# Expert down product as three passes of the rounded format, with w_down split ahead of the expert stage

## What is computed

```
for e in range(N_EXPERTS):
    h = jax.nn.silu(xt @ w_gate[e]) * (xt @ w_up[e])
    out = out + comb[:, e:e + 1] * (h @ w_down[e]).astype(f32)
```

## Time and profile before

| | us |
|---|---|
| median of 3 runs | 1359.34 |
| lowest and highest | 1359.04, 1362.73 |
| the profiled execution | 1360.82 |
| its span, first to last instruction | 1359.2 |

### The profile page before, as it was taken

The page is one execution under the profiler, slowest core; times in us unless marked ns, Lnnn a source line. Parts: engine busy times, 40 slices in busy tenths (PEclk is TensorE's granted clock), DMA queues, the critical chain, the costliest instruction groups (busy, mean ns, idle before and its releaser), DMA issues. The chain is left out here.

```text
span 1359.2 us, 22656 instructions
## 1 busy us (share of the span) xinstructions
PE 1198.9 (88%) x6653; PEld 957.0 (70%) x6654; DVE 893.2 (66%) x1975; ACT 462.5 (34%) x696; POOL 486.3 (36%) x557
## 2 busy tenths in 40 slices
PE   7999999799979768999999269999999999999910
PEld 6997999778767534888888257767767767767600
DVE  3452866468877573466667667777777777777586
ACT  4121010110012451222221225556556555556433
POOL 3008850210110033322322233545545545445267
PEclk9999899899979998999999579999999999999965
DMA  8555352564155322433332546787877777644484
GB/s 257 172 199 156 105 166 63 145 231 183 63 154 157 104 96 67 152 112 112 120 119 98 223 164 192 216 244 225 253 203 227 211 210 217 144 98 98 112 318 171
DMA packets 112875, 222.84 MB, mean 164 GB/s; under 512 B 51305, under 2 KB 68281, under 8 KB 103569
## 3 DMA queue, kind: packets, MB, share of 16 engines
q1 hardware_dynamic: 96368, 164.86, 36.3%
q0 software_dynamic: 15408, 55.12, 17.5%
q10 hardware_dynamic: 1040, 2.10, 0.4%
HBM read 144.34 MB, written 77.58 MB: 163 GB/s over the span
## 5 line engine op out<-in xcount | busy, mean ns | idle before, releaser
L2057 DVE TENSOR_TENSOR wgu<-w_raw,wgu (+1 forms) x192 | 226.0, 1219 | 52.5 <-ACT wgu L2144 52.5
L2244 PE MATMUL p_gu<-wgu,xg_high 128*128 x768 | 254.5, 413 | 4.5 <-DVE xg_low L2050 4.5
L2144 ACT CAST wgu<-w_raw (+1 forms) x192 | 187.1, 1050 | 19.4 <-SPq L1865 16.7
L2244 PEld LDWEIGHTS p_gu<-wgu,xg_high 128*128 128x128 f32 x768 | 145.2, 191 | 59.1 <-issue 31.3
L2267 PE MATMUL p_d<-wd,ht 128*128 x384 | 174.9, 598 | 1.8 <-DVE ht L2071 1.0
L2244 PE MATMUL p_gu<-wgu,xg_low 128*128 x384 | 152.0, 396 | 0.0
L2267 PEld LDWEIGHTS p_d<-wd,ht 128*128 128x128 f32 x384 | 69.0, 189 | 71.5 <-issue 71.2
L1730 PE MATMUL p_out<-w_out_high,mixt_high 128*128 128x512 f32 (+1 forms) x272 | 108.6, 399 | 10.5 <-POOL mixt_low L1507 10.5
L1730 PE MATMUL p_out<-w_out_high,mixt_low 128*128 128x512 f32 (+1 forms) x272 | 106.9, 393 | 0.0
L1730 PE MATMUL p_out<-w_out_low,mixt_high 128*128 128x512 f32 (+1 forms) x272 | 106.8, 393 | 0.0
L1936 POOL TENSOR_TENSOR spare_e<-nothing 128x1 f32<-128x1 f32 x48 | 9.3, 194 | 232.2 <-DVE yo L2077 232.2
(11 more groups left out here) (434 smaller groups left out, 2689.0 us busy)
## 6 DMA issues: line engine op xcount, KB each, us to landing
w_raw<-in_w_gate SPq DMA_DIRECT2D x16, 1024.0 KB, 4.8
w_raw<-in_w_up SPq DMA_DIRECT2D x16, 1024.0 KB, 7.7
wd<-in_w_down SPq DMA_DIRECT2D x16, 1024.0 KB, 4.7
acc_rows<-ax SPq DMA_DIRECT2D x18, 512.0 KB, 5.7
xin<-in_x_prompt SPq DMA_DIRECT2D x16, 512.0 KB, 6.3
sq<-sq_mats SPq DMA_DIRECT2D x16, 512.0 KB
z<-in_x_prompt SPq DMA_DIRECT2D x16, 512.0 KB, 4.2
x_rows<-x SPq DMA_DIRECT2D x16, 512.0 KB, 4.9
```

The source lines that it names most:

```text
L2057: low = tt(wgu[:, slot, 1, at], raw[:, slot, at], wgu[:, slot, 0, at].bitcast(F32), ALU.subtract)
L2144: nc.scalar.copy(wgu[:, slot, 0, at], raw[:, slot, at]).then_inc(hi_set, 1)
L2244: mm = t.matmul(pg[b][:, :, :], x[:, b, k, :], w[h][:, k], start=(k == 0 and x is xh and h == 0), stop=(k == KD - 1 and x is xl))
```

## The change

The down product becomes three passes of the rounded format. In detail:

- Both parts of w_down, high and low, are made ahead of stage E and kept in DRAM (`wd_dram`). The work comes in 64 units of 128 x 512 (a quarter of an expert, 256 KB): 32 in stage A, 8 in stage B, 24 in stage D. A unit is a load by SP, a cast by ACT, a subtraction (DVE in A and D, POOL in B) and two stores by SP.
- In stage A a unit lives in two buffers of x rows that become free (`xin` keeps two for the rows from tile 6 on) or in parts of `ya` not yet written. A static list places up to two units in each of the steps 4 to 22; a unit listed at step n is worked on in step n+1. By the list, twelve units are worked on in steps 16 to 23. ACT does its cast behind the u tile's evacuation, DVE its subtraction behind the xs tile's.
- In stage D the units live in the parts of `ya` and `yb` that tiles already read; two a tile. In stage B they have a buffer of their own, and ACT's loop is written out.
- In stage E `wd` has a high and a low half for each of two experts, loaded by two transfers of 1 MB instead of one. `ht` is split too: ACT casts (`hidden_high`), DVE subtracts.
- `turn_hidden(i-1)` moves from behind `gate_up(i)` to its middle. ACT does `hidden_high` between its third and fourth cast.
- The two rows of the second norm (`g2_row`, `b2_row`) are loaded near the end of the tiles instead of at the start of stage E; small tables move.

```diff
+            UNITS, busy = [], {}
+            for n in range(FT, 27):
+                free = [s for s in SLOTS if busy.get(s, 0) <= n and n + 3 <= SLOTS[s]]
+                free.sort(key=lambda s: (s[0] == "x", SLOTS[s]))
+                for s in free[:2 if n % 2 or 8 <= n else 1]:
+                    if len(UNITS) < 32:
+                        UNITS.append((n, s))
+                        busy[s] = n + 3
...
                 def u_tile(i, f):
                     act.wait_ge(u_prod, i * FT + f + 1)
...
+                    for j, s, m in units_at(i * FT + f - 1):
+                        act.wait_ge(wd_ld[s], m * 16 + 16)
+                        nc.scalar.copy(wd_part(s, 1, True), wd_part(s, 0, False)).then_inc(wd_high, 1)
...
+                    for j, s, m in units_at(i * FT + f - 1):
+                        dve.wait_ge(wd_high, j + 1)
+                        v.tensor_tensor(wd_part(s, 0, True), wd_part(s, 0, False), wd_part(s, 1, True).bitcast(F32),
+                                        ALU.subtract).then_inc(wd_low, 1)
...
                 def down(e):
-                    sp.dma_start(wd[:, 1 - e % 2, :], a["w_down"][0, expert(e)].rearrange("(p k) f -> p (k f)", p=P)).then_inc(wd_in[e % 2], 16)
+                    for h in range(2):
+                        sp.dma_start(wd[h][:, 1 - e % 2, :].bitcast(F32), wd_dram[h][expert(e)]).then_inc(wd_in[e % 2], 16)
...
                 def tail(i, b, first):
-                    dve.wait_ge(h_turned, i + 1)
-                    v.tensor_copy(ht[:, b], pt_h[:, :, :]).then_inc(ht_set, 1)
+                    dve.wait_ge(ht_high, i + 1)
+                    tt(ht[1][:, b], pt_h[:, :, :], ht[0][:, b].bitcast(F32), ALU.subtract).then_inc(ht_set, 1)
...
+                def hidden_high(i, b, first):
+                    act.wait_ge(h_turned, i + 1)
+                    if not first:
+                        act.wait_ge(d_prod, i)
+                    nc.scalar.copy(ht[0][:, b], pt_h[:, :, :]).then_inc(ht_high, 1)
...
                         prep(i, not begun and b == 0, slot, ready)
+                    if begun or b:
+                        hidden_high(i - 1, 1 - b, not begun or begun == 1 and b == 0)
+                    if not last:
+                        high(slot, range(3, 4))
...
                     for k in range(KD):
+                        if k == KD // 2 and between:
+                            between()
...
                     for m in range(2):
                         for k in range(2):
-                            mm = t.matmul(pd[m][:, :], ht[:, b, k, :], w[:, k, m * SUP:(m + 1) * SUP], start=(k == 0), stop=(k == 1))
+                            for x, h in PARTS:
+                                mm = t.matmul(pd[m][:, :], ht[x][:, b, k, :], w[h][:, k, m * SUP:(m + 1) * SUP],
+                                              start=(k == 0 and x + h == 0), stop=(k == 1 and x == 1))
```

More of the change, by code:

```diff
@@ L136, in hybrid_step @@
         x1_dram = dram("x1_rows", [SEQ + NS, D])
+        wd_dram = [dram(f"w_down_{n}", [E, P, 4 * SUP]) for n in ("high", "low")]
+        wd_src = a["w_down"][0].rearrange("e (p k) (h f) -> e p (k h) f", p=P, h=2)
         acc_dram = dram("acc_rows", [SEQ + NS + 2 * P, D])
@@ L266, in _ @@
                             sp.dma_start(sq_dram[pair, :, 0, :], s_mat[:, pair % 2, :]).then_inc(s_stored[pair % 2], 16)
+                        units(n)
+                        if i and f % 2 and 2 * i + 4 + f // 2 < CH:
+                            rows_in(2 * i + 4 + f // 2)
+                for s in SLOTS:
+                    sp.wait_ge(wd_st[s], sum(u[1] == s for u in UNITS) * 32)
                 sp.wait_ge(kz, 1)
@@ L784, in hybrid_step @@
             xv_in = [phase_sem(f"xv_in{i}") for i in range(2)]
+            wd_ld, wd_st = ([phase_sem(f"b_wd_{k}{s}") for s in range(3)] for k in ("in", "stored"))
+            wd_high, wd_low = sems("b_wd_high b_wd_low")
             LAG = 3
@@ L821, in _ @@
                 sp.wait_ge(vs_stored, 16)
+                for s in range(3):
+                    sp.wait_ge(wd_st[s], (3, 3, 2)[s] * 32)
                 sp.wait_ge(toep_in, L * 16)
@@ L859, in _ @@
                 nc.scalar.activation(vs[:], psv[:, :], ACT.Gelu_apprx_tanh).then_inc(vs_gelu, 1)
[L860 to L864, removed]
+                for c in range(4, CH):
+                    gelu(c, c % 4, False)
             @block.vector
@@ L1491, in _ @@
                         stores(i * 2 + b, b)
+                        units_out(i - 1 + b, 1 - b)
+                        units_in(i, b)
                 rows_in(CH - 2, 0)
-                for p in range(CH - 2, CH + 1):
-                    stores(p, p % 2)
+                stores(CH - 2, 0)
+                units_out(CH // 2 - 2, 1)
+                units_in(CH // 2 - 1, 0)
+                stores(CH - 1, 1)
+                units_out(CH // 2 - 1, 0)
+                stores(CH, 0)
+                sp.wait_ge(wd_st[0], 6 * 64)
+                sp.wait_ge(wd_st[1], 6 * 64)
                 for s in (x1_stored, ax1_stored):
@@ L1586, in score, with units @@
                     nc.scalar.activation(scores[0:n, tile_row, :], prt[0:n, :], ACT.Sigmoid).then_inc(r_set, 1)
+                def units(i, b):
+                    act.wait_ge(wd_ld[b], i * 32 - 32 * (1 - b))
+                    for at in areas(i * 2 + b):
+                        nc.scalar.copy(yb_r[:, :, at], ya[:, :, at]).then_inc(wd_high, 1)
                 high(0, 0, True, NS)
@@ L1595, in _ @@
                 score(0, NS)
-                with act.Fori(1, CH // 2 - 1) as i:
+                for b in range(2):
+                    high(4 + b, b)
+                    tile(2 + b, b, 1)
+                    score(1 + b)
+                units(1, 1)
+                with act.Fori(2, CH // 2 - 1) as i:
                     for b in range(2):
@@ L1604, in _ @@
                     score(p - 1)
+                    if p == CH - 2:
+                        units(CH // 2 - 1, 0)
                 score(CH - 1)
@@ L1806, in hybrid_step @@
             hh = sb("hh", [P, 2, FF], where=pt)
-            ht = sb("ht", [P, 2, 2, P], where=pt)
+            ht = [sb(f"ht_{n}", [P, 2, 2, P], F32R, where=pt) for n in ("high", "low")]
+            assert pt.at <= base + 32 * KB
             pt = Place(nc, base + 35 * KB)
@@ L2139, in turn_b, with high @@
                         nc.scalar.copy(xh[:, b, h * 4:h * 4 + 4, :], pt_x[h]).then_inc(xt_hi, 1)
-                def high(slot):
-                    for c in range(4):
+                def high(slot, cs=range(4)):
+                    for c in cs:
                         at = slice(c * QG, (c + 1) * QG)
@@ L2232, in turn, with gate_up @@
                     mm.then_inc(x_turned, 1)
-                def gate_up(i, b, first):
+                def gate_up(i, b, first, between):
                     slot = pe.value_load(tab[0:1, 0, bass.ds(i, 1)], min_val=0, max_val=1)
```

155 lines of the change are left out of this document (129 added, 26 removed).

## The result

The changed kernel takes **1441.88 us** (median; 1441.62 to 1442.52), the kernel before beside it 1359.19: a ratio of 1.060, 95% interval 1.0585 to 1.0621, slower. The profiled execution spans 1440.0 us, against 1359.2, at a mean granted clock of 0.909, against 0.943. The forecast was 1349.

The account below looks back on a forecast made before the run. The prediction took PE to bound stages A, D and E, and B nearly so. From 1359.2 us, -23.0 (down product) +0.5 (end of E) +10 (A) +1.5 (B) +1 (D) gave 1349, range 1333 to 1364.

Parts of the forecast that it names:

- Stage E: Expert stage: three passes make the down product 2.74 instead of 3.46; 32 steps gain 0.72, -23.0 us, and +0.5 at the end.
- rival (4): Stage E: expert changes don't hold PE because the split gets done sooner; -34.6 and +13, 1338 us; chance 0.08.
- rival (5): Stage E: the transposes within gate and up cost their bound of 7 us; 1356 us; chance 0.07.
- The rule of four passes: Stage E's down product: full FP32 counts as four array passes, so three passes take 2.60 and gain 27.5 us.
- Transfers in E at 0: Stage E: two MB of w_down an expert instead of one cost nothing; bound 10 us.
- Rival (2): Stage E: DMA binds, two-tile experts taking 21.0 instead of 19.6 us; +10, 1359 us; chance 0.13.
- Stage D at +1 with a bound of 5: Stage D: 24 units on ACT and DVE, behind PE's 235.6 us of work, cost +1 us; bounds 0 and 5.
- Stage A at +10, bounds 0 and 40: Stage A: 0 before step 16; in steps 16 to 23 5 us, plus one or two clock falls of 3.4 each.
- the prediction's own signs: Stage A: PE idle before pst behind v_im, and the clock; a stage of 260 to 280 confirms, 290 is rival (1).
- rival (1): Stage A goes late: DVE's v_pair ends behind PE's projection, PE idles, clock falls; 1369 us at +30; chance 0.14.
- the rule of contention that was weighed for A: Stage A: POOL contends with DVE's two-input unit subtractions, which take about double; some 7 us more.
- Stage B at +1.5, bound 5: Stage B: eight units, casts on ACT, subtractions on POOL at 1.3 each, cost +1.5 us; bounds 0 and 5.

Follow-up runs that it names:

- e8: The kernel without any units, with the SiLU rows' transposes and ACT's high copy put back behind gate and up and the fourth cast: 1352.82 us, against 1336.74 without that.
- e2: The changed kernel with stage D's two unit loads per tile issued ahead of the row stores and unit stores: 1385.86 us.
- e4: The changed kernel without stage A's unit stores; units still loaded, cast and subtracted, stage E loads those experts' w_down itself: 1412.13 us.
- e7: e5 plus one more tile step between load and cast of stage A's units, loads ahead of stores, two more free regions of ya: 1359.34 us.
- e5: e2 plus one wait in stage B: POOL's unit subtraction waits until DVE has written vn of the same tile: 1380.52 us.
- e3: The changed kernel without stage A's unit casts and subtractions; SP waits for each landing and stores the raw unit twice: 1410.38 us.

## Why the prediction was wrong

**Stage E, right in its mechanism and its total.** 48 down products lost 0.66 each (3.46 to 2.80, 0.06 less than forecast, which took gate and up's 0.228 for each matmul). Steps with the same expert behind one of the same are 9.43 (forecast 9.35). A change and the step behind it took 10.6 and 9.75 before, 10.20 and 9.54 after: 0.61 for the two together, where 0 and 0.72 were forecast. E and the end together came to -21.6, forecast -22.5, which agrees better than its parts: from first to last gate and up it was -19.5 (forecast -23.0), behind the last -2.1 (forecast +0.5). That changes still wait for DVE's quarter is in the chain above; rival (4) falls. Moving the transposes cost nothing (2.75+0.23+2.75), so rival (5) falls, and e8 shows the move itself worth 16. The rule of four passes (the Trainium skill, FP8 and Floating Point Precision, TensorE Precision Notes), which gave -27.5, overshoots: by it the product would take 2.60, and it took 2.80.

**Transfers in E at 0, right.** In the changed kernel's stage E neither PE nor ACT has a wait for a transfer; SP's longest waits for wd and raw landings were 11.1 and 10.8 us. Rival (2) falls.

**Stage D at +1 with a bound of 5: the step that failed.** The prediction compared busy time (ACT 48.7 and DVE 142.9 of 245) and said that SP's new waits are "met by work that doesn't wait for SP". The wait that mattered is not SP's but ACT's, for the unit's landing, and it was nowhere in the text, nor was what is queued behind it: the cast of mixt, then POOL's mixt_low, root, x1, and with x1 SP's own next loads. The landing waits for SP, SP for x1, x1 for ACT. With a ring the question is how long it takes, 19 us, against PE's 13.3; the six store issues inside it, 5.5 us from 709.69 to 715.23, decided, and e2 took them out. It came to +55.6. Half of that is the lower clock, which the prediction reckoned in A alone.

**Stage A at +10, bounds 0 and 40: the path was right, the wait at its head had no price.** It came to +34.6. By the prediction's own signs (a stage of 290, PE idle in front of pst behind v_im) that is rival (1), which had 0.14. The u tiles of the two kernels are level up to tile 9, 11.6 us apart at tile 15 (116.9 and 128.5), ahead of the first pair, and 34.1 apart at tile 23 (193.2 and 227.4). So a third of the loss comes before step 16, where the prediction took 0, in part in windows where POOL does nothing:

```profile
80.00:100.00 20.00, 16.31 (x126) 16.11 (x125) 13.88 (x73) 5.48 (x11) 0.00 (x0) 0.92 1.06 346
```

Nearly all the rest comes in steps 16 to 23, where the prediction had looked, and in the place that it named. PE's waits for v_im before and after (us in total, times, longest us):

```profile
PE pst L646 <- DVE v_im L566: 2.3, 2, 1.9
```
```profile
PE pst L708 <- DVE v_im L628: 14.8, 5, 5.3
```

(The 5.3 in five of the prediction counts the waits of PE and of its weight loads together.) One of them in the changed kernel's timeline:

```profile
213.18 0.62 ACT L413 CAST ya_r<-ya 128x512 fp32r<-128x512 f32 x1 [9.44 <-DMA ya<-in_w_down]
213.83 0.69 DVE L488 TENSOR_TENSOR ya_r<-ya,ya_r 128x512 fp32r<-128x512 f32 x1 [9.34 <-ACT ya_r L413]
...
216.97 0.42 DVE L628 TENSOR_TENSOR v_im<-tv 128x256 f32<-128x256 f32 x1
...
217.44 0.47 PE L708 MATMUL pst<-ident,v_re 128*128 128x128 f32 x1 [5.24 <-DVE v_im L628]
```

The products of v_pair are not slow (v_re 424 ns in the median); they start late, because DVE stands behind ACT's cast and ACT behind the landing. The prediction had drawn this order and priced DVE's 0.61 in it, not the wait for a transfer that has one step of 7 us, while 25 MB were added to a stage whose DMA share was already 0.49 to 0.52. The work by itself costs 3 (e4). Here the lower clock took less than in D: PE's matmuls were busy 9.4 us longer (250.2 against 240.9), the other 25 us are idle time.

DVE's unit subtractions in A took 0.90 and 0.94 in the mean, where the same form took 0.68 in stage D (forecast 0.61, half of a longer one); one in e7, beside POOL's pairs, took 3.31:

```profile
123.70 3.31 DVE L492 TENSOR_TENSOR ya_r<-ya,ya_r 128x512 fp32r<-128x512 f32 x1 [0.43 <-ACT ya_r L417]
```

So the rule of contention that was weighed for A (the Trainium skill, GPSIMD Engine Reference, the row on SBUF interfaces) holds in kind; that it costs the stage 7 us doesn't, since in e4 all the work cost it 3.

**Stage B at +1.5, bound 5: too low; it came to 7.3.** Contention was weighed for A and not for B, where POOL's work was put just where it lets DVE go; that was 3.6 (e5). **Stage C and the lists** moved by 1.2 and 3.6, taken at 0 without a word; why was not traced. In e2 D's tail and the lists take 58.3, less than before.

**The range.** Its upper end came from rival (1) alone. Nothing in it stood for a stage that turns from PE-bound to bound by a ring of waits.

## What to carry to other kernels

Work that is given to an idle engine is free only if nothing that the full engine needs stands behind its waits: ask for each new wait what stands behind it in that engine's order, and follow it round until it comes back to the transfer that it waits for. Where it does, the length of the ring against the loop's period decides, not the busy shares; issue loads ahead of stores and leave a full step more between load and use. Where PE is full, an idle stretch costs more than itself, since a lower clock followed: as much again in stage D (27.6 and 28.5 us), a third as much again in stage A (25 and 9.4).

## What was not expected of the hardware

- A DMA share of 1.04 over 140 us (e3) cost PE nothing, at a granted clock of 0.99; landings of 6.3 us in the median, and issues of unit stores of up to 9.43, did no harm where only SP waited.
- A vn on DVE with one tensor input took 1.50 beside a POOL subtraction of 1.29, against 0.55 alone; the pair all but ran one after the other.
- SP took 0.5 us to issue most unit stores of stage A, but 5.45 behind a store of u blocks, and 3.77 and 3.80 in e2. Why was not tested.
- About half of stage D's loss was lower clock and not idle time: 1170 matmuls at 0.89 were busy 28 us longer than 1167 at 0.99. In stage A it was about a quarter.
